# Fox and dilated hybrid decoder step: output turns due later, memory norm's turns moved, waits of TensorE split or moved

## What is computed

```
xn = rmsnorm(x, g_mix);  z = xn @ w_in          # fox q, k, v, forget gate; dilated q, k, v; two gates
o_fox  = forgetting attention, 8 heads          # samples: over 16 cached pages of 128 rows + 8 new rows
o_dil  = three windows (128/1, 512/4, 2048/16), 4 heads each, merged by their denominators
merged = sigmoid(g_fox) * (o_fox @ w_br_fox) + sigmoid(g_dil) * (o_dil @ w_br_dil)
x += merged @ w_mix_out
x += cross_attn(rmsnorm(x, g_xattn), rmsnorm(mem, g_mem) @ w_xkv)   # 256 memory rows, 4 heads
x += conv_ffn(rmsnorm(x, g_ffn))                # w_up, 3-tap conv, gelu(gate) * val, w_down
y = rmsnorm(x, g_final)
```

## Time and profile before

| | us |
|---|---|
| median of 3 runs | 2770.35 |
| lowest, highest | 2768.77, 2773.72 |
| the profiled execution | 2772.53 |
| its span, first to last instruction | 2770.7 |
| TensorE busy in it | 2728.6 |
| VectorE, ScalarE, GpSimd busy | 1151.3, 528.3, 145.4 |
| mean granted clock of TensorE | 0.993 |

### The profile page before, as it was taken

One profiled execution on the slowest core, in us unless ns is written; L12 is line 12 of the kernel. 1 busy time (PEld: TensorE's weight loads), 2 busy tenths in 40 slices (PEclk: granted clock), 3 DMA queues, 4 the chain that ended last, 5 costly groups with the idle time before them and its releaser, 6 DMA issues.

```text
span 2770.7 us, 37655 instructions
## 1 busy us (share of the span) xinstructions
PE 2728.6 (98%) x14274; PEld 1857.1 (67%) x14274; DVE 1151.3 (42%) x2788; ACT 528.3 (19%) x1160; POOL 145.4 (5%) x268
## 2 busy tenths in 40 slices
PE   8999999999999999999999999999999999999998
PEld 7655556767655555456644577546888888888887
DVE  2255543332253233333264023345666666654432
ACT  2233323221201112111002112221112112210002
POOL 1000001020101112100000000000000000000000
PEclk9999999999999999999899999999999999999999
DMA  5000102000116778865511400333445433152201
GB/s 189 22 13 9 59 24 65 28 19 20 44 27 198 214 212 262 244 202 171 200 66 61 152 31 31 130 130 115 140 128 172 149 118 125 46 170 91 82 29 65
DMA packets 207160, 294.48 MB, mean 106 GB/s; under 512 B 20781, under 2 KB 145086, under 8 KB 205942
## 3 DMA queue, kind: packets, MB, share of 16 engines
q1 hardware_dynamic: 148150, 187.76, 20.9%
q10 hardware_dynamic: 42976, 89.26, 10.1%
q0 software_dynamic: 15856, 15.07, 2.2%
HBM read 268.07 MB, written 63.35 MB: 120 GB/s over the span
## 4 chain that ended last, share of the span: by engine, by line
PE 96%; DMA 2%; DVE 1%; issue 1%; ACT 0%; SPq 0%; ACTq 0%; DVEq 0%
PE psum L2518 20%; PE psum L955 11%; PE psum L2898 10%; PE psum L1864 9%; PE psum L531 5%; PE psum L2202 4%; PE psum L1948 4%; PE psum L2049 3%; PE psum L702 3%; PE psum L1287 3%; PE psum L718 3%; PE psum L1872 3%; PE psum L1323 3%; PE psum L1303 2%; PE psum L2176 2%; PE psum L729 2%
## 5 line engine op out<-in xcount | busy, mean ns | idle before, releaser
L2518 PE MATMUL psum<-arena 128*128 128x272 f32 x2464 | 567.3, 394 | 0.5 <-DVE arena L2592 0.5
L2518 PEld LDWEIGHTS psum<-arena 128*128 128x128 f32 x2464 | 470.2, 191 | 97.0 <-issue 0.6
L955 PE MATMUL psum<-arena 128*128 128x512 f32 (+3 forms) x960 | 316.9, 481 | 1.4 <-ACT arena L584 1.4
L1864 PE MATMUL psum<-arena 128*128 128x368 f32 (+1 forms) x768 | 298.2, 489 | 1.4 <-DVE arena L1807 1.2
L2898 PE MATMUL psum<-arena 128*128 128x256 f32 (+1 forms) x1584 | 288.1, 356 | 0.0
L2898 PEld LDWEIGHTS psum<-arena 128*128 128x128 f32 (+1 forms) x1584 | 252.8, 178 | 34.3 <-issue 3.2
L955 PEld LDWEIGHTS psum<-arena 128*128 128x128 f32 (+1 forms) x960 | 195.1, 250 | 62.3 <-issue 35.1
L778 DVE CUSTOM_DVE_ANT_0 arena<-psum,arena 128x256 f32<-128x256 f32 (+2 forms) x224 | 95.4, 457 | 207.0 <-PE psum L702 206.6
L1864 PEld LDWEIGHTS psum<-arena 128*128 128x128 f32 x768 | 123.2, 190 | 68.2 <-issue 42.1
L2621 DVE TENSOR_TENSOR arena<-arena,psum 128x272 f32<-128x272 f32 (+2 forms) x330 | 111.7, 377 | 112.8 <-PE psum L2518 112.0
L752 ACT ACTIVATE arena<-arena 128x256 f32<-128x256 f32 (+4 forms) x192 | 107.5, 562 | 228.7 <-DVE arena L778 227.2
(11 more groups left out here) (242 smaller groups left out, 2973.7 us busy)
## 6 DMA issues: line engine op xcount, KB each, us to landing
arena<-in_cache_fox_kv ACTq DMA_DIRECT2D x128, 256.0 KB, 4.3
arena<-in_cache_fox_kv SPq DMA_DIRECT2D x128, 256.0 KB, 4.4
out_win_s<-in_cache_win_kv ACTq DMA_DIRECT2D x8, 4080.0 KB, 15.4
arena<-in_w_up SPq DMA_DIRECT2D x44, 512.0 KB, 6.3
arena<-in_w_down SPq DMA_DIRECT2D x14, 1408.0 KB, 6.3
arena<-in_cache_win_kv SPq DMA_DIRECT2D x16, 1024.0 KB, 7.9
arena<-in_cache_mem_kv SPq DMA_DIRECT2D x16, 1024.0 KB, 6.3
arena<-in_w_in SPq DMA_DIRECT2D x9, 1024.0 KB, 7.8
```

What stands on the lines that cost most here:

```text
L955: last = pe.matmul(banks[c0 // 512][p0:p0 + r, 0:n], xn_tile(k, g, t), wD[g][:, k, w0:w0 + n], start=(k == 0), stop=(k == KD - 1))
L1864: last = pe.matmul(banks[0][:, 0:cw], w[:, k, :], xnT[:, k, c0:c0 + cw], start=(k == 0), stop=(k == KD - 1))
L2518: last = pe.matmul(bank_of(j, x, p), w[:, k, :], r[:, k, Q4 * p:Q4 * p + Q4], start=(k == 0), stop=(k == 3))
```

## The change

Five edits.

1. The last TensorE waits before dilated group 0 are placed where their operand is first read or overwritten: the first matmul into bank 0 waits for all but the last copy, the first into bank 1 for all, the first turn through bank 2 for the kept keys.
2. Fox output turns O get offset 24 in place of 20: behind the next sample's P turns.
3. w_br_dil gets a semaphore of its own, and TensorE waits for it before the second branch.
4. Stage nm is (1484, 1498) in place of (1478, 1490).
5. The p4 units do columns 256 to 511 first and 0 to 255 last. For the last tile ScalarE squares columns 256 to 1023 as soon as they are final, turns that sum into a bias (Identity with scale 1/D plus eps), and then squares only columns 0 to 255.

```diff
--- before.py
+++ after.py
@@ -145,7 +145,7 @@
     p1=(112, 174), a0=(114, 176), p2=(174, 236), a1=(178, 238), p3=(236, 298), a2=(240, 300),
     d0=(298, 440), a3=(302, 372), b0=(380, 480), d1=(440, 580), b1=(500, 612), d2=(580, 715), b2=(640, 752),
     combine=(776, 860), ga=(715, 1010), gb=(1010, 1448), foxprep=(765, 775), fox=(869, 1223), dilprep=(1226, 1228),
-    dil=(1230, 1422), gs=(1450, 1464), mix=(1464, 1576), nm=(1478, 1490), n2=(1554, 1608),
+    dil=(1230, 1422), gs=(1450, 1464), mix=(1464, 1576), nm=(1484, 1498), n2=(1554, 1608),
     memkv=(1577, 1636), q=(1650, 1814), x=(1692, 1856), c=(1848, 2040), n3=(1880, 2066), xp=(1872, 2012))
 
 
@@ -938,8 +938,6 @@
             now = at(f"d{g}")
             if g == 0:
                 yield now(0)
-                pe.wait_ge(fp["copied"], 4 * PAIR)
-                pe.wait_ge(fp["k_kept"], 12)
             for t in range(TT):
                 r = rows_of(t)
                 for c0, cw, part in ((0, 512, 0), (512, 256, 0.62)):
@@ -949,6 +947,8 @@
                         if k == 0:
                             if t == 0 and c0 == 0:
                                 pe.wait_ge(s["w_in"], z["w_in"] + 48)
+                            if t == 0 and g == 0:
+                                pe.wait_ge(fp["copied"], 4 * PAIR - (0 if c0 else 1))
                             if g or t:
                                 pe.wait_ge(*nth(dp[g], "v_copied" if c0 else "roped", t))
                         for p0, w0, n in sides:
@@ -964,6 +964,8 @@
         def dil_turn(pe, g, t):
             s, z = dp[g]["s"], dp[g]["z"]
             pe.wait_ge(s["roped"], z["roped"] + t + 1)
+            if g == 0 and t == 0:
+                pe.wait_ge(fp["k_kept"], 12)
             if g or t:
                 pe.wait_ge(s["kept"], z["kept"] + t)
             for j in range(4 if t < NQ else 2):
@@ -1567,7 +1569,7 @@
             landed(eng, fv_in[n % NVR], n // NVR + 1)
 
         fox_split = [[p] for p in range(NPG - 1)] + [[NPG - 1, NPG]]
-        fox_tail = [("P", q, 2 + q) for q in range(5)] + [("V", p, 4 + 15 * p // 16) for p in range(NPG)] + [("O", 0, 20)]
+        fox_tail = [("P", q, 2 + q) for q in range(5)] + [("V", p, 4 + 15 * p // 16) for p in range(NPG)] + [("O", 0, 24)]
         pg_fox = paged(fox_turns, fox_groups, P, kts_f, s_fox, NPG + 1, fox_p_keep, fox_pv, fox_split, o_fox, 1, stats_f,
                        pair_out(oTf, 4), fox_tail, PLAN["fox"],
                        dict(turn=banks[2:4], score=banks[4:6], tail=banks[6], o_ps=banks[7][:, 0:P]), add_ready=fox_add_ready)
@@ -1815,6 +1817,7 @@
         sgs = take(2 * KD * SM, f0 + 32768).rearrange("p (a m c) -> p a m c", a=2, m=KD)
         w_bs = take(6 * D, f0 + 8192).rearrange("p (k n) -> p k n", k=6)
         gw_s, gw_z = again("weights", "in0 in1", lambda n: 32 * KD)
+        ws_dil = ring([0] * 8 + [1])[8]
         gt = sems("gates", "ws_in computed opened branched gated merged s_computed s_gated s_merged")
         w_bf = I["w_br_fox"][0].rearrange("(k p) n -> p k n", p=P)
         w_bd = I["w_br_dil"][0].rearrange("(k p) n -> p k n", p=P)
@@ -1842,7 +1845,7 @@
             yield PLAN["dil"][1] + 1
             pages_over(sp, pg_dil)
             sp.dma_start(w_bs[:, 0:4, :], w_bf).then_inc(gt["ws_in"], 16)
-            sp.dma_start(w_bs[:, 4:6, :], w_bd).then_inc(gt["ws_in"], 16)
+            sp.dma_start(w_bs[:, 4:6, :], w_bd).then_inc(ws_dil[0], 16)
 
         def gates_pe(pe):
             for u in range(N_GU):
@@ -1873,10 +1876,12 @@
                 last.then_inc(gt["computed"], 1)
             yield at("gs")(0)
             pages_over(pe, pg_dil)
-            pe.wait_ge(gt["ws_in"], 32)
+            pe.wait_ge(gt["ws_in"], 16)
             pe.wait_ge(gt["opened"], N_GU)
             pe.wait_ge(gt["gated"], N_GU)
             for a, (_, _, kn, oT) in enumerate(PASSES):
+                if a == 1:
+                    landed(pe, ws_dil, 1)
                 for m in range(KD):
                     for k in range(kn):
                         last = pe.matmul(banks[a][:, m * SM:(m + 1) * SM], w_bs[:, 4 * a + k, m * P:(m + 1) * P], oT[:, k, S:TOK],
@@ -2754,7 +2759,7 @@
                 d_units += [(name, c, t) for t in range(4)]
                 d_units += {"p1": [("b11", c, 0)], "p2": [("b21", c, 0)], "p3": [("b22", c, 0)]}.get(name, [])
                 d_units += {("p2", 1): [("b12", 0, 0)], ("p7", 0): [("b12", 1, 0)]}.get((name, c), [])
-        d_units += [("p4", c, t) for t in range(4) for c in range(2)]
+        d_units += [("p4", c, t) for t in range(4) for c in (1, 0)]
         NU_D = len(d_units)
 
         def unit_done(name, c, t=None):
@@ -2772,7 +2777,8 @@
         slot_in = dict(zip(("x0", "x1", "x2", "m0", "m1", "m2"), down_in))
         rows_in = down_in[6:9]
         w_dn = I["w_down"][0].rearrange("(f p) n -> p f n", p=P)
-        ln_s, ln_z = again("norm", "", lambda n: TT if n in ("squared", "rooted", "inverted") else 0)
+        ln_s, ln_z = again("norm", "", lambda n: TT + (2 if n == "squared" else 0) if n in ("squared", "rooted", "inverted") else 0)
+        part_ssq, part_bias = ssq[:, TT * 5 - 1:TT * 5], std[:, TT * 5 - 2:TT * 5 - 1]
         ln = dict(s=ln_s, z=ln_z)
         s_out = sem("y_ready")
         s_y = sem("y_stored")
@@ -2904,19 +2910,28 @@
         LC = 3 * TT + 2
         row_done = {t: unit_done("p3", 1, t) for t in range(4)}
         row_done[NQ] = unit_done("b22", 1)
-        row_done.update({4 + t: unit_done("p4", 1, t) for t in range(4)})
+        row_done.update({4 + t: unit_done("p4", 0, t) for t in range(4)})
         row_order = sorted(row_done, key=lambda t: row_done[t])
 
         def down_act(act):
             act.wait_ge(*nth(dn, "computed", unit_done("p6", 1)))
             for i, t in enumerate(row_order):
                 r = rows_of(t)
+                bias = eps_t[0:r, :]
+                if t == NQ - 1:
+                    act.wait_ge(*nth(dn, "added", row_done[t] - 1))
+                    act.activation(sq[:, CW:D], x_res[:, t, CW:D], ACT.Square,
+                                   accum_out=part_ssq).then_inc(ln["s"]["squared"], 1)
+                    act.wait_ge(*nth(ln, "squared", i + 1))
+                    act.activation(part_bias, part_ssq, ACT.Identity, bias=eps_t, scale=1.0 / D).then_inc(ln["s"]["squared"], 1)
+                    bias = part_bias
                 act.wait_ge(*nth(dn, "added", row_done[t]))
-                act.activation(sq[0:r, :], x_res[0:r, t, :], ACT.Square,
+                now = slice(0, CW) if t == NQ - 1 else slice(0, D)
+                act.activation(sq[0:r, now], x_res[0:r, t, now], ACT.Square,
                                accum_out=ssq[0:r, LC + t:LC + t + 1]).then_inc(ln["s"]["squared"], 1)
-                act.wait_ge(*nth(ln, "squared", i + 1))
+                act.wait_ge(*nth(ln, "squared", i + (3 if t == NQ - 1 else 1)))
                 act.activation(std[0:r, LC + t:LC + t + 1], ssq[0:r, LC + t:LC + t + 1], ACT.Sqrt,
-                               bias=eps_t[0:r, :], scale=1.0 / D).then_inc(ln["s"]["rooted"], 1)
+                               bias=bias, scale=1.0 / D).then_inc(ln["s"]["rooted"], 1)
 
         def h_sum(dve, n):
```

## The result

| | before | after |
|---|---|---|
| median of 5 runs, us | 2770.35 (2767.88 to 2773.72) | 2755.88 (2755.18 to 2756.42) |
| ratio, 95% interval | | 0.9942 (0.9927 to 0.9957) |
| the profiled execution, its span | 2772.53, 2770.7 | 2755.18, 2753.4 |
| TensorE busy | 2728.6 | 2717.2 |
| mean granted clock | 0.993 | 0.998 |

A forecast was written before the change was run, and what follows sets the result against it. TensorE, busy for 98% of the span, was taken to bound the kernel. Terms 1.4 + 2.7 + 0.9 + 0.5 + 1.7 + 0.6 = 7.8 us off the 2770.35 median gave 2762.5 us, range 2757 to 2767.5.

The forecast's parts named there:

- the long stretch: Over the branches: 20.48 us at half clock, put down to the 64-column matmuls and left as it was, no gain.
- rival (c): Over the branches: the 20.48 us half-speed stretch goes or shrinks, up to 9 us, down to 2753.6; chance 0.12.
- The forecast's own sign for being wrong: TensorE: pauses fall by under 3 us, or the half-speed stretch of 20 us changes by more than 4.
- Edit 1, 1.4: Start of dilated group 0: TensorE's pause of 1.43 us goes, lower bound 0.6.
- Edit 2, 2.7: Fox stage: five P-turn waits on the output copy, 870 to 1140 us, go; 2.7 us, from 0 to 3.3.
- The sixth pause: Fox stage behind 1140 us: P-turn pause of 0.6 us, given no gain because page waits there would grow.
- rival (b): Fox stage: page waits take back 2.7 us and the fox weight isn't ahead, 0.9 less; time 2766.1, chance 0.15.
- Edit 3, 0.9: Ahead of the branches: 0.9 of TensorE's 1.55 us pause goes, then the last gate result binds; bounds 0 and 1.5.
- Edit 4, 0.5: Memory norm turns: a new 1.9 us pause replaces the 2.43 us one, net 0.5, from -1 to 2.4.
- Clock under s, 1.7: s matmuls at the memory norm: 3.42 us at half clock goes, gain 1.7 us, bounds 0 and 1.7.
- rival (a): Memory norm: the new pause draws the clock down as the old did, 3.4 us at half; time 2764.2, chance 0.20.
- Edit 5, 0.6: End of the kernel: the last square over fewer columns saves 0.6 us, bounds 0.5 and 0.7.

The follow-up runs named there:

- double: combo with every branch matmul computed twice over, the result the same; high launches 2762.9 us (nine).
- after2: The changed kernel once more, without an edit; median 2757.7 us of 9, ratio to the kernel before 0.9953.
- combo: Changed kernel with nm at (1484, 1494) and the wait for the last gate result behind the first branch; median 2752.4 us of 6, ratio to before 0.9937.
- long: Kernel before, with the branches also waiting for the first half of w_mix_out; median 2785.6 us of 7, ratio 1.0051.

## Why the prediction was wrong

The step that failed is the last sentence on the clock, which puts the long stretch at nothing: "The longer stretch at half, 20.48 us over the branches, I leave as it is: it began 2.5 us after the pause of 1.55 and went on for 15 us of L1882 without a pause, so it comes from those 64-column matmuls." That 15 us of them ran without a pause and stayed low shows that they don't raise the clock. I read it as that they lower it, which is another claim, and `double` refutes it. The cause was the pause of 1.55 us ahead of them, which edit 3 cut to 0.72. The forecast gave that edit 0.9 us for the pause; the clock behind it was worth 9.4 between the two profiles. The mechanism stood there as rival (c), up to 9 us, with a chance of 0.12. The forecast's own sign for being wrong came true: the 20 us stretch changed by more than 4, and TensorE's busy time fell by 11.4, not by 1.7, while the pauses fell by 5.9 with 5.5 forecast.

The second half of the mistake is that one profile was taken for the kernel. The kernel before runs in two kinds of launches 7 to 8 us apart (2774.9 and 2767.0, 2774.5 and 2766.8, 2774.7 and 2767.7 on three chips), and the profile was of the low kind. The spread of the runs shown, 5 us, was in the text, but only as width for the range. On a mean over launches the stretch is worth 7.5 x 38 / 80 = 3.6 us, an estimate from those medians. With the 8.6 of the other terms below that is 12.2, and `after2` beside before gave 11.5. That the recorded comparison gave 14.5 is in part the chance of which five launches of before it held.

Point by point:

- **Edit 1, 1.4:** right, 1.43 in the profile, and nothing took its place. That VectorE's L606 and not the named L584 was the releaser rests on the times in the earlier trace rows alone: the edit moves both waits, and no run moves one of them.
- **Edit 2, 2.7:** 3.2. The sixth pause was not taken back by the pages; the page waits were 6.3 after and 6.2 before, so rival (b) had nothing in it. The fox stage as a whole got only 1.5 us shorter in this execution (below).
- **Edit 3, 0.9:** 1.55 - 0.72 = 0.8, and the new releaser is VectorE's last gate result, as worked out. The fox weight landed 8.2 us after its issue, the other 10.3 after its own (7.7 and 9.9 before), in order of issue again. The Trainium skill (DMA: Bandwidth & Descriptors, Queues, rings and completion order) says that completion isn't in order of issue for loads of one engine; for this pair no profile here shows it.
- **Edit 4, 0.5:** 2.43 - 1.75 = 0.7. The new pause is where it was put, 0.15 shorter than worked out. That a pause returns, and of this size, came from counting what VectorE has ahead of the second tile.
- **Clock under s, 1.7:** right, 1.9 (9.01 us of s before, 7.09 after), and the new pause of 1.75 didn't bring the stretch back. All six profiles with the old pause there (2.4 to 3.0 us, ahead of turns of 128 columns) have a stretch of 3.41 us at half behind it, none of the seven without it has one. So rival (a) is out. In combo, where the new pause goes too, nothing more is gained there in clock.
- **Edit 5, 0.6:** right, 0.64.
- **The long stretch, 0:** 7.5 + 1.9 = 9.4 us between the two profiles. This is what was missed.

The first six sum to 1.4 + 3.2 + 0.8 + 0.7 + 1.9 + 0.6 = 8.6 with 7.8 forecast, and with 9.4 to 18.0. The spans differ by 17.3, and the same records laid beside each other say where. Up to the last matmuls of L1131 (L1133 now) ahead of the fox stage the changed kernel is 1.7 us ahead:

```profile
829.29 2.79 PE L1131 MATMUL psum<-arena 128*64 128x512 f32 x12
...
827.58 2.79 PE L1133 MATMUL psum<-arena 128*64 128x512 f32 x12
```

At the last gate matmuls it is 3.2 ahead (1356.21 against 1352.98), so the fox stage gave 1.5 and not 3.2; its two stretches at half, 6.8 us in all, can have cost up to 3.4. The branches, the mix product and the norm gave 12.7 (12.8 by the terms). Behind 1890 us a short stretch at half was 3.4 us long in place of 6.8, and 0.8 more came off there, and 0.6 at the end. That makes 17.3.

The Trainium skill (TensorE: Matmul & The Clock Gate, Why this matters for your kernels) warns of pauses longer than the 1.55 us. The 7.65 us of `long` agree with it, low in 7 of 7. But a pause of 1.55 to 1.74 us was enough in half of the launches, where narrow matmuls followed, and there the measurement decides.

## What to carry to other kernels

When the granted clock is at half over some stage, ask separately what let it fall and what fails to bring it back. A pause of a microsecond or two ahead of narrow matmuls can cost many times its length, and the place to look is the pause before the stretch, not the work in it. When TensorE is busy for 98% of a span, also compare its busy time at an equal count of records: if that falls and no instruction changed, look at the clock. And before a sum is made on one profile, lay the mean clock of that execution beside those of the other runs.

## What was not expected of the hardware

- By its mean clock, the same kernel on the same chip has the long half-speed stretch in about half of its launches (16 of 35, 10 of 23, 12 of 22). The profiles with a pause of 1.55 to 1.74 us are of both sorts, four with the stretch and two without, at pauses that hardly differ. Between 0.73 and 1.55 the share goes from 1 of 26 to half, and at 7.65 it is 7 of 7. Nothing between was tried.
- Once at half, 64-column float32 matmuls back to back stay there for 15 to 20 us; once at full, they stay there for 21.5.
- In the row of L1882 the pair of a weight load and 64 columns takes 0.11 us at full and 0.21 at half, so the whole pair goes with the clock.
